# Paired experts: the small expert's up copy and the gated values go ahead of the second up rounding on ScalarE

## The chip, the cores and the metric

The kernel runs on one core of one Trainium2 chip. The metric is the device time of one execution in microseconds; the time before is the median of three runs. Five engines work side by side, each through its own queue in order, and wait for each other by semaphores: TensorE (PE in the profile, PEld for its weight loads), VectorE (DVE), ScalarE (ACT), GpSimd (POOL) and SyncE (SP), which here issues the transfers of the weights.

## The reference

Four layers on 256 tokens of width 1024, in two blocks. The stage that matters here is the mixture of experts in the second layer:

```
def swiglu(x, w1, w3, w2):
    return (jax.nn.silu(x @ w1) * (x @ w3)) @ w2

def moe_swiglu(x, w_router, w1, w3, w2):
    ...
    logits = (t @ w_router).astype(jnp.float32)
    top_val, top_idx = lax.top_k(logits, TOP_K)
    top_w = jax.nn.softmax(top_val, axis=-1)
    combine = jnp.sum(jax.nn.one_hot(top_idx, N_EXPERTS, dtype=jnp.float32) * top_w[..., None], axis=1)
    out = jnp.zeros_like(t)
    for e in range(N_EXPERTS):
        out = out + combine[:, e:e + 1].astype(t.dtype) * swiglu(t, w1[e], w3[e], w2[e])
    return out.reshape(bn, s, d)
```

There are 8 experts with two chosen for each token, and a hidden width of 3584. Every number is float32, so all of an expert's weights come from memory once, whoever uses them: 42 slots of 1 MB for each expert, 336 in all.

## The kernel before

**Pairs and steps.** The experts are handled in four pairs: of each pair one expert has many tokens (up to 128) and one has few (up to 64). The hidden width is cut into 14 chunks of 256 columns, so there are 4 x 14 = 56 steps (`PAIR_STEPS`). In a step s the core needs six slots of weights, 128 x 2048 numbers each: two up slots and one down slot of the "many" expert, and the same of the "few" expert.

**Two ways to multiply.** The few expert's products run in plain float32 on the slots as they lie in the ring. The many expert's run as three products of rounded numbers each: every weight w is split in a high part (w rounded, made by ScalarE into a buffer that the profile calls `work_rounded`) and a low part (w minus the high part, made by VectorE in place in the ring, `ring_rounded`). The same is done with the gated values (`ff_hid_rounded`, high and low part).

**The ring.** SP issues one transfer for each slot into a ring of six (`ring`, L732, `expert_slot`). Before the issue of slot n it waits until TensorE has used slot n - 6, in the order of use; `weights_used` counts the slots that TensorE is done with. The slots of a step stand in the order many up (two halves), few down of the step before, few up (two halves), many down of the step before. The two halves of many up for step s + 1 are the last two of the six that are wanted while step s is under way.

**TensorE**, for a step s, runs in this order (L1896 on, all recorded by helper line L1392, the turn at L1936):

```
                for s in range(1, PAIR_STEPS):
                    many_up(s)
                    few_down(s - 1)
                    few_up_products(s)
                    many_turn(s)
                    many_down(s - 1)
                    few_turn(s)
                    side(s)
```

`many_up` (24 matmuls, two halves of 12; each half needs the low part of its slot, and its end releases the slot), `few_down` and `few_up_products` (`ring` as an operand), `many_turn` (a transpose of the gated values of 128 tokens), `many_down` (12 matmuls with `ff_hid_rounded`), `few_turn` (eight 64-column products of `h_heads,hT`; it waits for the few expert's up copy, `few_up_here`, and for the low part of the gated values, `many_hid_low`), and `side`, which in up to eight of the 14 steps of a pair gathers tokens, turns, or scatters results.

**ScalarE** (`paired_experts`, L1022 on), in the profile's lines: L1052 silu of the few expert (`h_heads`), L1045 high part of the many down slot, L1058 silu of the many expert (`ff_silu`; it waits for the end of `many_up(s)`), L1038 high part of an up slot of step s + 1 (`up_high_of`, once for each half, each waiting for its landing), L1064 the few expert's up products copied out of PSUM (`few_up_of`, tile `hT`; it waits for the end of `few_up_products(s)` and for the few turn of the step before), L1070 high part of the gated values (`hid_high_of`; it waits for `many_turn(s)`).

**VectorE** (`paired_experts`, L2679 on, recorded by helper line L2262) makes the low parts in an order of its own: gated values of the many expert (`ff_mid`), low part of the first up slot of step s + 1 (`ring_rounded`), low part of the gated values (`ff_hid_rounded`), low part of the second up slot, later the few expert's gated values (`h_heads`) and the low part of the many down slot.

The orders are written out by hand, one after the other; no scheduler moves anything. In the printed code `up_high[s % 2][half]`, `down_high`, `few_up`, `ff_hid_r` and `ring_r` are the buffers `work_rounded`, `work_rounded`, `hT`, `ff_hid_rounded` and `ring_rounded` of the profile.

Of the kernel before, what the change touches and what calls it, by code (L numbers as in the profile page):

```python
# [34 lines left out]
PAIR_STEPS = PAIRS * EXPERT_CHUNKS  # L35
# [149 lines left out]
def build_program(nc, x_in, cond_in, params_in, consts_in, stream_in, out, plan=PLAN):  # L185
# [6 lines left out]
    with ExitStack() as ctx:  # L192
# [48 lines left out]
        def bank(i, a=0, b=512):  # L241
            if i in banks:
                return banks[i][:, a:b]
            two, half = (mid, i - 2) if i < 4 else (pair, i - 6)
            return two[:, 512 * half + a:512 * half + b]
# [399 lines left out]
        def pair_used(s, what, half=0):  # L645

            return weights_used, moe_first + pair_slot(s, what) + half + 1

        def pair_here(s, what, half=0):

            at = moe_first + pair_slot(s, what) + half
            return weights_here[at % RING], 16 * (at // RING + 1)

        def pair_ring(s, what, half=0):

            return (moe_first + pair_slot(s, what) + half) % RING
# [214 lines left out]
        def _(act):  # L871
# [150 lines left out]
            def paired_experts():  # L1022
# [11 lines left out]
                def up_high_of(s, half):  # L1034
                    act.wait_ge(*pair_here(s, "many", half))
                    if s >= 2:
                        act.wait_ge(*pair_used(s - 2, "many", half))
                    act.activation(up_high[s % 2][half], ring[:, pair_ring(s, "many", half), :], ACT.Copy)\  # L1038
                       .then_inc(many_up_high, 1)

                def down_high_of(s):
                    act.wait_ge(*pair_here(s, "many_down"))
                    if s >= 2:
                        act.wait_ge(*pair_used(s - 2, "many_down"))
                    act.activation(down_high[s % 2], ring[:, pair_ring(s, "many_down"), :], ACT.Copy)\  # L1045
                       .then_inc(many_down_high, 1)

                def silu_of_few(s):
                    act.wait_ge(few_turned, s + 1)
                    if s >= 2:  # L1050
                        act.wait_ge(few_hid_here, s - 1)
                    act.activation(few_silu[s % 2], bank(6, T, T + P), ACT.Silu).then_inc(few_silu_here, 1)  # L1052

                def silu_of_many(s):
                    act.wait_ge(*pair_used(s, "many", 1))
                    if s >= 2:
                        act.wait_ge(many_hid, s - 1)
                    act.activation(ff_silu[:, s % 2, :], bank(4, 0, T), ACT.Silu).then_inc(many_silu, 1)  # L1058

                def few_up_of(s):  # L1060
                    act.wait_ge(*pair_used(s, "few", 1))
                    if s:
                        act.wait_ge(few_turned, s)
                    act.activation(few_up, bank(5), ACT.Copy).then_inc(few_up_here, 1)  # L1064

                def hid_high_of(s):
                    act.wait_ge(many_turned, s + 1)
                    if s >= 2:
                        act.wait_ge(*pair_used(s - 2, "many_down"))
                    act.activation(ff_hid_r[:, s % 2, :], bank(6, 0, T), ACT.Copy).then_inc(many_hid_high, 1)  # L1070
# [14 lines left out]
                def evacuate_side(s):  # L1085
                    p, c = divmod(s, EXPERT_CHUNKS)
                    if c == 0 and p:
                        outs(p - 1)
                    if c == 7:
                        act.wait_ge(pair_turned, p + 1)  # L1090
                        if p:
                            act.wait_ge(pair_scattered, 4 * p)
                        act.activation(pair_back, bank(7), ACT.Copy).then_inc(pair_backs, 1)
                    if p + 1 < PAIRS and c in (8, 9):
                        many_tokens_of(p + 1, c - 8, 7)
                    if p + 1 < PAIRS and c == 10:
                        few_tokens_of(p + 1, 7)
# [6 lines left out]
                for s in range(PAIR_STEPS):  # L1104
                    if s:
                        silu_of_few(s - 1)
                        evacuate_side(s - 1)
                        down_high_of(s - 1)
                    silu_of_many(s)
                    if s + 1 < PAIR_STEPS:  # L1110
                        for half in range(2):
                            up_high_of(s + 1, half)
                    few_up_of(s)
                    hid_high_of(s)
                silu_of_few(PAIR_STEPS - 1)
                down_high_of(PAIR_STEPS - 1)
                outs(PAIRS - 1)
# [253 lines left out]
            for n, kind in enumerate(plan):  # L1371
                norm(n, 0)
                if kind.startswith("first"):
                    first_mixers(firsts.index(n))
                elif kind == "even":
                    even_mixers(n)
                else:
                    odd_mixers(n)
                norm(n, 1)
                if kind == "first1":  # L1380
                    router(n)
                    paired_experts()
                    with act.If(more_tokens(act)):
                        experts_again()
                    norm(n, 2)
                else:
                    feed_forward(n, kind)
# [1934 lines left out]
```

## Time and profile before

| | us |
|---|---|
| median of 3 runs | 2489.4 (2487.48 to 2495.14) |
| profiled execution, its own time | 2496.13 |
| its span | 2494.3 |
| TensorE busy | 2365.2 (95%) |
| VectorE busy | 1477.3 (59%) |
| ScalarE busy | 970.3 (39%) |
| read from memory | 653.76 MB, mean 263 GB/s over the span |

The busy shares are means over the whole span. Matmuls overlap, so a busy TensorE isn't TensorE at its peak. The stage of the paired experts fills the time from about 600 to 1530 us after the start; in it a row of the timeline gives the start of an instruction, how long it took, its line and tiles, and in brackets how long its engine had been idle and what ended that. A chain of waits is followed back from the last instruction to what released it, step by step.

### The profile page before, as it was taken

How to read it: one execution, taken by the hardware profiler on the slowest of the kernel's cores; microseconds unless marked ns; L12 is line 12 of the kernel's file. 1: busy time of each engine (PE TensorE's matmuls, PEld its weight loads, DVE VectorE, ACT ScalarE, POOL GpSimd, SP SyncE). 2: the span in 40 equal slices, each digit the busy share in tenths (PEclk: the TensorE clock that was granted, in tenths of full speed). 3: DMA queues.
4: the chain of work that ended last, by engine and by line, in shares of the span. 5: the costliest groups of instructions: out<-in, count | busy, mean ns of one | idle time of the engine just before them, and what ended most of it. 6: DMA issues, size and time to landing. Idle time of an engine off the chain costs nothing.

```text
span 2494.3 us, 36105 instructions
## 1 busy us (share of the span) xinstructions
PE 2365.2 (95%) x14484; PEld 1922.5 (77%) x14484; DVE 1477.3 (59%) x1843; ACT 970.3 (39%) x1149; POOL 44.8 (2%) x37
## 2 busy tenths in 40 slices
PE   5999999998999999989999998999999999999999
PEld 4889998876566565656665665779899999997998
DVE  5835885764444454444544444375489887873665
ACT  3214434113434444343434434222434456653332
POOL 0100001000000000000000000010000000000000
PEclk9989999999999999999999999999999999999999
DMA  9845894746989999989989999230488543432452
GB/s 369 330 152 203 358 364 179 304 152 262 366 349 366 368 364 359 364 348 369 363 338 382 362 374 371 107 118 1 154 330 360 210 169 136 149 139 101 155 184 100
DMA packets 90428, 656.78 MB, mean 263 GB/s; under 512 B 10033, under 2 KB 10289, under 8 KB 10801
## 3 DMA queue, kind: packets, MB, share of 16 engines
q1 hardware_dynamic: 80928, 589.34, 61.2%
q10 hardware_dynamic: 9360, 65.52, 6.4%
q8 instruction: 97, 1.59, 0.2%
q14 instruction: 43, 0.34, 0.0%
HBM read 653.76 MB, written 1.05 MB: 263 GB/s over the span
## 4 chain that ended last, share of the span: by engine, by line
PE 78%; DMA 9%; DVE 6%; issue 3%; ACT 3%; ACTq 0%; SPq 0%; DVEq 0%
PE bank L1392 77%; DMA ring<-stream_dram 9%; DVE work L2274 1%; DVE ring_rounded L2262 1%; ACT hT L1064 1%; DVE ff_hid_rounded L2262 1%; DVE rstd L2322 0%; PE bank L1936 0%; DVE xT L2268 0%; ACT ff_hid_rounded L1070 0%; DVE ring L2274 0%; PE bank L1772 0%; DVE ff_mid L2268 0%; ACT work_rounded L1038 0%; DVE yT L2268 0%
## 5 line engine op out<-in xcount | busy, mean ns | idle before, releaser
L2262 DVE TENSOR_TENSOR ring_rounded<-ring,work_rounded 128x2048 fp32r<-128x2048 f32 x264 | 606.4, 2298 | 461.6 <-ACT work_rounded L1045 347.7
L1392 PE MATMUL bank<-work_rounded,proj_rounded 128*128 128x512 f32 x896 | 310.2, 418 | 1.5 <-DVE ring_rounded L2262 1.5
L1392 PE MATMUL bank<-h_heads_rounded,work_rounded 128*128 128x256 f32 x1344 | 278.9, 280 | 0.0
L1392 PE MATMUL bank<-yT_rounded,ring_rounded 128*128 128x256 f32 x960 | 273.6, 285 | 0.0
L1038 ACT ACTIVATE work_rounded<-ring 128x2048 fp32r<-128x2048 f32 x112 | 214.7, 1918 | 131.5 <-DMA ring<-stream_dram 131.0
L1392 PE MATMUL bank<-hT,ring 128*128 128x256 f32 x1088 | 242.9, 383 | 2.0 <-ACT hT L926 2.0
L1392 PEld LDWEIGHTS bank<-hT,ring 128*128 128x128 f32 x1088 | 207.5, 192 | 37.7 <-issue 9.9
L1392 PEld LDWEIGHTS bank<-h_heads_rounded,work_rounded 128*128 128x128 f32 x1344 | 220.6, 189 | 3.0 <-issue 2.9
L1045 ACT ACTIVATE work_rounded<-ring 128x2048 fp32r<-128x2048 f32 x56 | 107.2, 1914 | 286.9 <-DMA ring<-stream_dram 281.5
L1392 PEld LDWEIGHTS bank<-work_rounded,proj_rounded 128*128 128x128 f32 x896 | 177.1, 198 | 42.4 <-issue 2.8
L1392 PE MATMUL bank<-ring,proj 128*64 128x512 f32 x896 | 201.8, 592 | 0.0
L1392 PEld LDWEIGHTS bank<-yT_rounded,ring_rounded 128*128 128x128 f32 x960 | 186.3, 194 | 0.0
L1392 PE MATMUL bank<-ring_rounded,proj_rounded 128*128 128x512 f32 x448 | 182.5, 407 | 0.0
L1392 PEld LDWEIGHTS bank<-ring,proj 128*64 128x64 f32 x896 | 64.2, 137 | 127.5 <-issue 127.4
L1392 PE MATMUL bank<-work_rounded,ff_hid_rounded 128*128 128x512 f32 x448 | 155.6, 408 | 1.9 <-DVE ring_rounded L2262 1.9
L1392 PE MATMUL bank<-yT_rounded,work_rounded 128*128 128x256 f32 x480 | 138.8, 289 | 10.3 <-DVE ring_rounded L2262 10.3
L1392 PE MATMUL bank<-proj_rounded,work_rounded 128*128 128x256 f32 x480 | 138.0, 287 | 0.0
L1392 PE MATMUL bank<-yT_rounded,proj_rounded 128*128 128x256 f32 x480 | 136.1, 284 | 1.5 <-DVE ring_rounded L2262 1.5
L1392 PE MATMUL bank<-proj_rounded 128*128 128x256 f32 x480 | 135.7, 283 | 0.0
L1392 PE MATMUL bank<-h_heads_rounded,ring_rounded 128*128 128x256 f32 x480 | 135.5, 282 | 0.0
L1392 PE MATMUL bank<-yT,ring 128*128 128x256 f32 x512 | 114.1, 380 | 6.6 <-DMA ring<-stream_dram 3.7
L1392 PE MATMUL bank<-hT_rounded,work_rounded 128*128 128x256 f32 x384 | 115.7, 301 | 1.5 <-DVE h_heads_rounded L2268 1.4
(329 smaller groups left out, 4161.7 us busy)
## 6 DMA issues: line engine op xcount, KB each, us to landing
ring<-stream_dram SPq DMA_DIRECT2D x561, 1024.0 KB, 6.9
work<-stream_dram ACTq DMA_DIRECT2D x56, 1024.0 KB, 9.1
params<-params_dram ACTq DMA_DIRECT2D x1, 1728.5 KB, 28.9
consts<-consts_dram ACTq DMA_DIRECT2D x1, 1568.0 KB, 37.7
cond<-cond_dram ACTq DMA_DIRECT2D x2, 512.0 KB, 3.7
xT<-x_dram ACTq DMA_DIRECT2D x1, 1024.0 KB, 10.1
out_dram<-xT SPq DMA_DIRECT2D x1, 1024.0 KB, 3.9
consts<-consts_dram ACTq DMA_DIRECT2D x1, 577.0 KB, 32.2
```

The costliest lines, as they stand in the source:

```text
L1038: act.activation(up_high[s % 2][half], ring[:, pair_ring(s, "many", half), :], ACT.Copy)\
L1045: act.activation(down_high[s % 2], ring[:, pair_ring(s, "many_down"), :], ACT.Copy)\
L1064: act.activation(few_up, bank(5), ACT.Copy).then_inc(few_up_here, 1)
L1392: return pe.matmul(o, lhsT=a, rhs=b, start=start, stop=stop, skip_group_check=True)
L2262: return dve.tensor_tensor(o, a, b, op)
L2274: last = dve.scalar_tensor_tensor(half, half, 1.0, row, ALU.mult, ALU.mult, accum_out=column(h))
```

## The change

In `paired_experts` on ScalarE the rounding of the second up slot of the next step (`up_high_of(s + 1, 1)`) is called after `few_up_of(s)` and `hid_high_of(s)` instead of ahead of them. The first one stays where it was. No other function and no other engine's code is touched.

```
                     if s + 1 < PAIR_STEPS:
-                        for half in range(2):
-                            up_high_of(s + 1, half)
+                        up_high_of(s + 1, 0)
                     few_up_of(s)
                     hid_high_of(s)
+                    if s + 1 < PAIR_STEPS:
+                        up_high_of(s + 1, 1)
                 silu_of_few(PAIR_STEPS - 1)
```

ScalarE in the paired experts, two steps running; a row is one or more instructions of a line, `work_rounded<-ring` at L1038 is the rounding of an up slot, `hT<-bank` the few expert's up copy, `ff_hid_rounded<-bank` the high part of the gated values. Before:

```order
L1058 ACTIVATE ff_silu<-bank 128x256
L1038 ACTIVATE work_rounded<-ring 128x2048 x2
L1064 ACTIVATE hT<-bank 128x512
L1070 ACTIVATE ff_hid_rounded<-bank 128x256
L1052 ACTIVATE h_heads<-bank 128x128
L1045 ACTIVATE work_rounded<-ring 128x2048
```

With the change:

```order
L1058 ACTIVATE ff_silu<-bank 128x256
L1038 ACTIVATE work_rounded<-ring 128x2048
L1064 ACTIVATE hT<-bank 128x512
L1070 ACTIVATE ff_hid_rounded<-bank 128x256
L1038 ACTIVATE work_rounded<-ring 128x2048
L1052 ACTIVATE h_heads<-bank 128x128
L1045 ACTIVATE work_rounded<-ring 128x2048
```

The second of the two roundings moved behind the two reads of PSUM; this repeats in 55 steps.

VectorE at the same place, of the changed kernel (the helper's line is one further down than before, 2263 for 2262): the product `ff_mid`, the low part of the first up slot, the low part of the gated values, the low part of the second up slot.

```order
L2263 TENSOR_TENSOR ff_mid<-bank4,ff_silu 128x256
L2263 TENSOR_TENSOR ring_rounded<-ring,work_rounded 128x2048
L2263 TENSOR_TENSOR ff_hid_rounded<-bank67,ff_hid_rounded 128x256
L2263 TENSOR_TENSOR ring_rounded<-ring,work_rounded 128x2048
L2263 TENSOR_TENSOR h_heads<-bank67,h_heads 128x128
```

Nothing moved here: the order is that of before.

## Rows read from the trace of the kernel before

**Rows 1.** The page: engines' busy time (share of span), and the chain by engine
```profile
PE 2365.2 (95%) x14484; PEld 1922.5 (77%) x14484; DVE 1477.3 (59%) x1843; ACT 970.3 (39%) x1149; POOL 44.8 (2%) x37
...
PE 78%; DMA 9%; DVE 6%; issue 3%; ACT 3%; ACTq 0%; SPq 0%; DVEq 0%
```

**Rows 2.** Windows: the stage, eight full us, a slow clock, an empty queue
```profile
core 0: us, PE busy (x) PEld busy (x) DVE busy (x) ACT busy (x) POOL busy (x), PEclk, DMA share, GB/s
600.00:1530.00 930.00, 880.39 (x4056) 562.29 (x4058) 434.29 (x380) 390.04 (x400) 0.00 (x0) 0.97 0.92 361
1067.00:1075.00 8.00, 5.86 (x30) 4.62 (x29) 5.12 (x4) 3.59 (x5) 0.00 (x0) 1.00 1.01 423
...
1108.00:1112.00 4.00, 4.00 (x16) 3.39 (x15) 1.98 (x2) 0.28 (x1) 0.00 (x0) 0.57 0.74 309
1113.00:1117.00 4.00, 4.00 (x19) 2.56 (x20) 0.71 (x1) 2.18 (x2) 0.00 (x0) 1.00 0.56 215
```

**Rows 3.** Waits from 600 to 1530 us: total us, times, longest
```profile
ACT work_rounded L1038 <- DMA ring<-stream_dram: 124.4, 105, 4.3
...
DVE ff_hid_rounded L2262 <- ACT ff_hid_rounded L1070: 64.3, 54, 2.4
PEld bank L1392 <- ACT hT L1064: 56.9, 28, 4.2
PE bank L1392 <- DVE ff_hid_rounded L2262: 46.5, 30, 4.0
PEld bank L1936 <- DVE ff_mid L2262: 25.8, 24, 2.3
```

**Rows 4.** Chain that ended last, in order of time: start, us, what
```profile
1060.99 7.15 DMA ring<-stream_dram
...
1069.98 0.58 ACT hT L1064
1070.56 0.28 ACT ff_hid_rounded L1070
1070.84 0.02 issue
1070.87 0.44 DVE ff_hid_rounded L2262
...
1071.44 6.77 PE bank L1392 x32
...
1078.37 7.17 DMA ring<-stream_dram
```

**Rows 5.** Timeline of ScalarE in the same step: start, us, instruction, [idle before]
```profile
1065.72 1.92 ACT L1038 ACTIVATE work_rounded<-ring 128x2048 fp32r<-128x2048 f32 x1 [2.87 <-DMA ring<-stream_dram]
1068.16 1.92 ACT L1038 ACTIVATE work_rounded<-ring 128x2048 fp32r<-128x2048 f32 x1 [0.52 <-DMA ring<-stream_dram]
1069.98 0.58 ACT L1064 ACTIVATE hT<-bank 128x512 f32<-128x512 f32 x1
1070.46 0.38 ACT L1070 ACTIVATE ff_hid_rounded<-bank 128x256 fp32r<-128x256 f32 x1
```

**Rows 6.** Timeline of VectorE in the same step
```profile
1067.67 2.29 DVE L2262 TENSOR_TENSOR ring_rounded<-ring,work_rounded 128x2048 fp32r<-128x2048 f32 x1 [2.42 <-ACT work_rounded L1038]
1070.87 0.42 DVE L2262 TENSOR_TENSOR ff_hid_rounded<-bank,ff_hid_rounded 128x256 fp32r<-128x256 f32 x1 [0.90 <-ACT ff_hid_rounded L1070]
1071.21 2.28 DVE L2262 TENSOR_TENSOR ring_rounded<-ring,work_rounded 128x2048 fp32r<-128x2048 f32 x1
```

**Rows 7.** Timeline of TensorE: end of many down, few turn, first matmul of many up
```profile
1068.91 0.39 PE L1392 MATMUL bank<-work_rounded,ff_hid_rounded 128*128 128x512 f32 x1
1071.44 1.08 PE L1392 MATMUL bank<-h_heads,hT 128*128 128x64 f32 x8 [2.14 <-DVE ff_hid_rounded L2262]
1072.32 0.47 PE L1392 MATMUL bank<-work_rounded,proj_rounded 128*128 128x512 f32 x1
```

**Rows 8.** Timeline of ScalarE in a step whose second up slot lands late
```profile
820.87 1.91 ACT L1038 ACTIVATE work_rounded<-ring 128x2048 fp32r<-128x2048 f32 x1 [0.75 <-DMA ring<-stream_dram]
824.83 1.91 ACT L1038 ACTIVATE work_rounded<-ring 128x2048 fp32r<-128x2048 f32 x1 [2.05 <-DMA ring<-stream_dram]
```

**Rows 9.** Timeline of TensorE in that step
```profile
825.43 0.39 PE L1392 MATMUL bank<-work_rounded,ff_hid_rounded 128*128 128x512 f32 x1
828.10 1.74 PE L1392 MATMUL bank<-h_heads,hT 128*128 128x64 f32 x8 [2.28 <-DVE ff_hid_rounded L2262]
829.60 0.77 PE L1392 MATMUL bank<-work_rounded,proj_rounded 128*128 128x512 f32 x1
```

## The prediction

> **What bounds the kernel now.** The page comes first: TensorE is busy for 95% of the span, and the chain that ended last lies 78% on it and 9% on transfers into the ring [rows 1]. Such shares are means over stages with different limits, so the second view is the table of windows. The diff touches the paired experts alone. Their stage runs from about 600 to 1530 us; TensorE is busy there for 880.39 of 930 us, and the DMA engines show a share of 0.92 at 361 GB/s [rows 2]. Two resources near their limits, tied by a ring of six slots: a slot is refilled only when TensorE has used it, and TensorE works only on what has landed and been rounded.
>
> The third view is the list of waits in that stage. TensorE waits 46.5 us in 30 places for `ff_hid_rounded` from VectorE, and its weight loads wait 56.9 us in 28 places for ScalarE's `hT` [rows 3]; both are the same point, the few turn (eight 64-column products), which needs the small expert's up copy (`hT`) and the low part of the gated values. VectorE in turn waited 64.3 us for the high part from ScalarE, and ScalarE's roundings of up slots waited 124.4 us for landings [rows 3]. So a landing that the few turn has no use for holds it up, through the order on ScalarE.
>
> The fourth view, the chain of one stretch, shows that this is a closed loop [rows 4]: 7.15 us from the issue of a slot to its landing, the rounding (shown as issue, as far as 1069.98), the up copy, the high part, the low part, then 6.77 us of TensorE (few turn and the next many up), whose end releases the slot for the next issue, 7.17 us to land, and so on. From 1060.99 to 1078.37 that is 17.4 us a step. TensorE's own work leaves out its 2.14 us wait [rows 7]; without that the step would be 15.2 us.
>
> **The change part by part.** It removes and adds no instruction; it moves the second up rounding behind the up copy and the high part, in 55 steps. No DMA is issued by ScalarE in this loop, and SP's, VectorE's and TensorE's orders stay.
>
> One step in numbers. Before, the roundings start at 1065.72 and 1068.16, the up copy at 1069.98 and the high part at 1070.46 [rows 5]; the low part starts at 1070.87 [rows 6], the few turn at 1071.44 [rows 7]. Counted from the second rounding's start the few turn is at +3.28 us.
> After, the first rounding ends at 1065.72 + 1.92 = 1067.64. The up copy can follow at about 1067.5 (its products are done, since many down has been running), the high part at 1068.0, ending at 1068.4. Now VectorE is late: in its order the low part of the first up slot, 2.29 us from 1067.67 to 1069.96 [rows 6], stands ahead of the gated values' low part. So that starts at 1069.9, and the few turn, 0.57 us behind it as before, at 1070.47. From the first rounding's start the few turn is at +4.75 us. The step gains 1071.44 - 1070.47 = 0.97 us of its 2.14; in general it gains the distance between the two roundings less 1.47 us, and never more than its wait.
>
> That distance is 2.44 us where two slots land back to back, and more where the second lands late: at 820.87 and 824.83 it is 3.96 us [rows 8]. There the few turn would be ready at 820.87 + 4.75 = 825.62, before many down ends at 825.82, and the wait of 2.28 us goes altogether [rows 9].
>
> Sum over the stage. I went through the steps one by one in the timeline: of the waits that stand in one row as 46.5 us, 30 times [rows 3], 19 are longer than 0.95 us with landings back to back and lose about 0.95 each (18.0); nine or ten are shorter and vanish (about 5); two have a late second landing and lose 2.28 and 1.90 (4.2). Together 27 us. About 19 us stay, bound by VectorE's rounding difference behind the first landing.
>
> What of the 27 us reaches the end? It does where the ring's next issue comes earlier and transfers follow. For: behind a long wait the DMA engines run dry, with a share of 0.56 at 215 GB/s, while they move 423 GB/s when slots are queued [rows 2]; at that rate the stage's 361 GB/s x 930 us would take 794 us, so there is room. Against: where slots are queued, an earlier TensorE only waits longer for the same landing. In my pass over the steps 15 us of the 27 fall directly ahead of a stretch with an empty queue, and 12 where one or two slots were still on their way. I take all of the first and two thirds of the second: 15 + 8 = 23 us.
>
> The clock adds to it. Behind some of the waits the granted clock falls to the lower of its two levels, 1.2 GHz: 0.57 on the mean of 1108 to 1112 [rows 2], and the first many-up matmul takes 0.77 us behind the wait at 828.10 [rows 9], against 0.47 us behind the one at 1071.44, which left the clock alone [rows 7]. The stage's mean of 0.97 [rows 2] is 3% of 930 us, some 28 us of TensorE's work. The drops stand behind waits of this kind, which shrink by a third to a half or go. This is bounded by 0 and 28 us; I take 4, near zero, since a wait of 2.14 us at 1071.44 and one of 2.28 us at 828.10 [rows 7, 9] had opposite outcomes.
> The Trainium skill ("TensorE: Matmul & The Clock Gate", HAM oscillation) says that waits for data between bursts bring the lower clock back each time and that shortening them keeps it away; by that rule this term would be nearer to its upper bound. The trace agrees only in part, since the wait of 2.14 us left the clock as it was.
>
> What the move costs. The second rounding now starts behind the high part: at 1068.40 instead of 1068.16 in this step, 0.24 us later, and it ends at 1070.3. VectorE takes it up at 1070.3 instead of 1071.21 [rows 6], because the gated values' low part stands ahead of it there and is now earlier. So the difference is done 0.9 us sooner than now, and the half of many up that reads it comes only 2.9 us after that product's start (it runs from 1072.32 [rows 7] to 1071.44 + 6.77 = 1078.21 [rows 4], in two equal halves). Cost here 0, covered by VectorE's own queue; what it costs without that cover is the first rival of the other sign. The wait for a landing that up copy and high part lose is taken over by the rounding itself, behind which stand now only the small expert's silu, which waits for the few turn anyway, and the down rounding, whose slot lands later still. ScalarE changes its function as often as before.
>
> Sum: 23 + 4 = 27 us. Against the profiled execution, 2496.13 us (span 2494.3), that gives 2469; it lay 6.7 us above the median of the runs shown, 2489.4, and against that the forecast is 2489.4 - 27 = **2462.4 us**.
>
> **The rivals.**
> (a) The transfers set the pace, and the gain is handed back as longer waits for landings. For it: a DMA share of 0.92 [rows 2], and ScalarE waits for the landing at 105 roundings of up slots [rows 3]. Against it: 423 against 361 GB/s, and the empty stretch [rows 2]. Time: unchanged, 2489 (within 5 us). The Trainium skill ("DMA: Bandwidth & Descriptors", Where 436 GB/s comes from) puts the limit of reads from HBM at about 358 GB/s for a core, by which the stage's 361 is already all there is and this rival is certain; the trace does not agree, as 8 us in a row ran at 423 GB/s. I give it 17%.
> (b) The loop itself gets shorter in each stalled step, so that the landings move too and the remaining 19 us of waits shrink as well, and the clock drops go. Loop through the first slot: 17.4 - 0.97 = 16.4 us. Price: 27 + 5 of the remaining waits + 12 of the clock = 44 us, 2445. The rows of the loop speak for it, the PE side work that several steps carry against it. 12%.
> (c) Slower: the second rounding queues behind the high part, which waits for TensorE's many turn. Where that turn is late, because VectorE's product for it is, the rounding of a slot that has long landed is held, then VectorE's difference, then the second half of the next many up. In the step above the difference is done at 1072.6 and needed at 1071.35 + 2.9 = 1074.25, so it decides from a turn that comes 1.7 us later than here. Where it does in one step of four by 0.7 us, 10 us are lost and little gained: 2499. Against it: the turn's weight loads wait 25.8 us in 24 places, 1.1 us on the mean and 2.3 at the longest [rows 3], mostly inside the slack. 5%.
> (d) The move doesn't take effect, because VectorE's first difference always ends after the second rounding would have. The rows exclude it for steps like these (1069.96 against 1070.84 for the end of the high part); it would give 2489, 2%.
>
> **How the numbers follow.** The forecast of 27 us, give or take 12, has 64%; (a) 17, (b) 12, (c) 5, (d) 2. The range: from (b)'s 2445 to just under the median, 2487, which leaves out most of (a)'s upper half and (c). A measurement of this kernel can tell about 0.3%, 7.5 us, from no change: faster than that is 2481.9 or less, the forecast and (b) with a little of (a), 0.77; the same 0.18; slower 0.05.
>
> **What would show it.** In the profile of the changed kernel, over the same stage: TensorE's wait for `ff_hid_rounded` falls from 46.5 us to 15 to 22, with a longest of under 3; the up copy's start follows the first rounding by about 1.8 us, and the few turn the first rounding's start by 4.75 us wherever it waits; VectorE's idle time before the gated values' low part goes nearly to nothing, since it comes straight from the first difference; GB/s of the stage rises from 361 to about 371; granted clock from 0.97 to 0.98. Wrong at its root: the wait shrinks and the stage is as long as before, with longer waits of ScalarE for landings (a); or a new wait of TensorE for `ring_rounded` inside many up (c).

## The result and the profile after

| | us |
|---|---|
| changed kernel, median of 4 runs | 2453.97 (2447.82 to 2459.84) |
| kernel before, median of the 4 runs beside them | 2488.44 (2482.43 to 2495.14) |
| ratio, changed to before | 0.9861, 95% interval 0.9822 to 0.9899 |
| profiled execution of the changed kernel, its span | 2450.09, 2448.3 |

The change takes 34.5 us off, 1.4% (interval 1.0 to 1.8%); 27 were forecast against 2489.4, and the median lies in the range. The two profiled executions differ by more, 2496.13 - 2450.09 = 46 us, since the one of before lay above its median and this one below. A second profile of the same changed kernel is at 2462.11 us (the run `e0_changed_again`, below), 34 us under before's; it is the highest of that run's six times, whose median is 2457.10. Where an amount matters both are given.

First the page of the changed kernel, engines' busy times and the chain by engine, which answer to [rows 1]. (The file is one line longer, so that TensorE's helper line is L1393, the turn L1937 and VectorE's helper L2263.)

```profile
PE 2341.7 (96%) x14484; PEld 1907.9 (78%) x14484; DVE 1475.2 (60%) x1843; ACT 967.9 (40%) x1149; POOL 44.7 (2%) x37
...
PE 72%; DMA 12%; DVE 7%; issue 4%; ACT 4%; ACTq 0%; SPq 0%; DVEq 0%
```

With the same instructions TensorE is busy for 23.5 us less, which shorter waits alone don't explain. Second, windows over the whole stage, from the first many up to the last many down: before, changed, changed again. The columns are those of [rows 2].

```profile
589.00:1562.00 973.00, 914.66 (x4212) 583.66 (x4213) 452.28 (x393) 409.59 (x420) 0.00 (x0) 0.97 0.92 362
```

```profile
587.00:1517.00 930.00, 892.07 (x4208) 570.46 (x4209) 450.57 (x394) 407.30 (x419) 0.00 (x0) 0.99 0.95 378
```

```profile
589.00:1529.00 940.00, 896.78 (x4208) 570.88 (x4208) 450.71 (x393) 406.02 (x419) 0.00 (x0) 0.99 0.95 374
```

The stage went from 973 us to 930 (940 in the second profile). That is 43 of the 46 us between the profiled executions (33 of the 34), so nearly all of the gain is in it. It splits in two: TensorE busy 914.66 to 892.07, 22.6 us less (17.9 in the second), and TensorE idle, length less busy, 58.3 to 37.9, 20.4 us less (15.1 in the second). The granted clock went from 0.97 to 0.99, the transfers from 362 to 378 GB/s (374).

Third, the waits in the changed kernel's stage that answer to [rows 3].

```profile
PEld bank L1937 <- DVE ff_mid L2263: 56.8, 40, 2.7
PE bank L1937 <- DVE ff_mid L2263: 22.7, 27, 1.8
PE bank L1393 <- DVE ff_hid_rounded L2263: 11.3, 13, 3.7
PE bank L1393 <- DVE ring_rounded L2263: 3.3, 3, 1.9
```

Two of the second profile:

```profile
PE bank L1393 <- DVE ff_hid_rounded L2263: 21.7, 23, 3.7
PE bank L1937 <- DVE ff_mid L2263: 18.1, 26, 2.6
```

And three of the kernel before, over the whole stage:

```profile
PE bank L1392 <- DVE ff_hid_rounded L2262: 47.4, 31, 4.0
PE bank L1936 <- DVE ff_mid L2262: 7.4, 11, 1.4
PE bank L1392 <- DVE ring_rounded L2262: 3.4, 3, 1.9
```

The few turn's wait is down from 47.4 us, 31 times, to 11.3 us, 13 times (21.7 us, 23 times, in the second profile), and no weight load waits for `hT` any more (56.9 us in [rows 3]). What grew is the many turn's wait for `ff_mid`: 22.7 us (18.1) in place of 7.4. The chain shows what it hangs on (start, us, what):

```profile
1051.48 8.39 DMA ring<-stream_dram
...
1059.89 1.92 ACT work_rounded L1045
...
1064.04 0.43 DVE ff_mid L2263
...
1064.52 0.44 PE bank L1937 x2
```

A transfer of 8.39 us, the high part of the down slot (L1045), its low part on VectorE (shown as issue), and only behind this, by VectorE's order, the gated values `ff_mid` that the many turn waits for. It is the same pattern one place further on: a landing for which the waiting product has no use, shown here in one step.

One step in the timeline, to set beside [rows 5 to 7]. ScalarE, VectorE, TensorE of the changed kernel:

```profile
1078.83 1.92 ACT L1038 ACTIVATE work_rounded<-ring 128x2048 fp32r<-128x2048 f32 x1 [1.83 <-DMA ring<-stream_dram]
1080.65 0.58 ACT L1064 ACTIVATE hT<-bank 128x512 f32<-128x512 f32 x1
1081.12 0.38 ACT L1070 ACTIVATE ff_hid_rounded<-bank 128x256 fp32r<-128x256 f32 x1
1081.39 1.92 ACT L1038 ACTIVATE work_rounded<-ring 128x2048 fp32r<-128x2048 f32 x1
```

```profile
1080.78 2.29 DVE L2263 TENSOR_TENSOR ring_rounded<-ring,work_rounded 128x2048 fp32r<-128x2048 f32 x1 [1.39 <-ACT work_rounded L1038]
1082.99 0.42 DVE L2263 TENSOR_TENSOR ff_hid_rounded<-bank,ff_hid_rounded 128x256 fp32r<-128x256 f32 x1
```

```profile
1083.55 1.08 PE L1393 MATMUL bank<-h_heads,hT 128*128 128x64 f32 x8 [0.75 <-DVE ff_hid_rounded L2263]
```

The few turn starts 1083.55 - 1078.83 = 4.72 us behind the first rounding (4.75 were forecast), and VectorE's difference is what it waits for, as the prediction had it. Every few turn that waits, except the first, lies at 4.72 or 4.73 us in the timeline of either profile of the changed kernel (the first at 4.71).

Last, where the busy time went. One row of the list of groups, the high-part products of many up, before and changed (count, then busy us and mean ns of one):

```profile
L1392 PE MATMUL bank<-work_rounded,proj_rounded 128*128 128x512 f32 x896 | 310.2, 418 | 1.5 <-DVE ring_rounded L2262 1.5
```

```profile
L1393 PE MATMUL bank<-work_rounded,proj_rounded 128*128 128x512 f32 x896 | 300.7, 407 | 1.5 <-DVE ring_rounded L2263 1.5
```

The same 896 matmuls take 9.5 us less. They are the product behind the few turn, where in [rows 9] the clock had fallen; none of them waited itself but for the 1.5 us in the row.

How much of the 22.6 us is the clock? In the stage, the traces' records of the granted clock have the lower level for 51.2 us in the kernel before, for 10.2 us in the changed one and for 13.7 in its second profile. At half the speed, 41 us less of it give back about 20 us (19 in the second profile; both are estimates from these lengths), which accounts for nearly all of the 22.6 us and for the 17.9. Each of the twelve drops of the kernel before begins behind a wait of TensorE of 1.5 to 4.0 us. The other runs agree: the mean granted clock of a whole execution was 0.975 to 0.983 in the 41 runs of the kernel before, with times from 2503.91 down to 2477.54 us, and 0.983 to 0.987 in the ten of the changed one. The means are 0.9797 and 0.9854, which over 2490 us is an estimated 14 us of the 34.5. The kernel before was profiled at 0.978, below its mean, so the profiles show the clock's part somewhat larger than the medians do.

Busy time isn't the clock alone: the few turn reads 1.08 us behind a wait [rows 7] and 1.00 without one, as in this row of the changed kernel's timeline. For 30 waits that is an estimated 2 us.

```profile
1051.14 1.00 PE L1393 MATMUL bank<-h_heads,hT 128*128 128x64 f32 x8
```

### The profile page after: what moved, and what is told of

It is laid out like the page before. It is cut to its first block, busy times and chain, and to the rows that moved or that the text cites. A ratio compares the mean times of both kernels' runs of the same rounds, so it can differ in the third digit from the quotient of the medians.

```text
span 2448.3 us, 36105 instructions
## 1 busy us (share of the span) xinstructions
PE 2341.7 (96%) x14484; PEld 1907.9 (78%) x14484; DVE 1475.2 (60%) x1843; ACT 967.9 (40%) x1149; POOL 44.7 (2%) x37
## 4 chain that ended last, share of the span: by engine, by line
PE 72%; DMA 12%; DVE 7%; issue 4%; ACT 4%; ACTq 0%; SPq 0%; DVEq 0%
PE bank L1393 71%; DMA ring<-stream_dram 11%; ACT work_rounded L1045 2%; DVE ring_rounded L2263 2%; DVE work L2275 1%; PE bank L1937 1%; ACT work_rounded L1038 1%; DMA work<-stream_dram 1%; DVE rstd L2323 1%; DVE ff_mid L2263 0%; DVE ff_mid L2269 0%; DVE xT L2269 0%; DVE ring L2275 0%; PE bank L1773 0%; DVE yT L2269 0%
## 5 line engine op out<-in xcount | busy, mean ns | idle before, releaser
L2263 DVE TENSOR_TENSOR ring_rounded<-ring,work_rounded 128x2048 fp32r<-128x2048 f32 x264 | 607.1, 2301 | 490.2 <-ACT work_rounded L1045 386.0
L1393 PE MATMUL bank<-work_rounded,proj_rounded 128*128 128x512 f32 x896 | 300.7, 407 | 1.5 <-DVE ring_rounded L2263 1.5
L1393 PE MATMUL bank<-h_heads_rounded,work_rounded 128*128 128x256 f32 x1344 | 279.0, 280 | 0.0
L1393 PE MATMUL bank<-yT_rounded,ring_rounded 128*128 128x256 f32 x960 | 273.7, 285 | 0.0
L1393 PE MATMUL bank<-hT,ring 128*128 128x256 f32 x1088 | 243.3, 384 | 2.0 <-ACT hT L926 2.0
L1038 ACT ACTIVATE work_rounded<-ring 128x2048 fp32r<-128x2048 f32 x112 | 214.7, 1917 | 61.8 <-DMA ring<-stream_dram 61.5
L1045 ACT ACTIVATE work_rounded<-ring 128x2048 fp32r<-128x2048 f32 x56 | 107.1, 1913 | 329.1 <-DMA ring<-stream_dram 329.0
L1393 PEld LDWEIGHTS bank<-hT,ring 128*128 128x128 f32 x1088 | 207.8, 192 | 37.8 <-issue 9.8
L1393 PEld LDWEIGHTS bank<-h_heads_rounded,work_rounded 128*128 128x128 f32 x1344 | 220.4, 189 | 3.0 <-issue 2.9
L1393 PE MATMUL bank<-ring,proj 128*64 128x512 f32 x896 | 201.8, 592 | 0.0
L1393 PEld LDWEIGHTS bank<-work_rounded,proj_rounded 128*128 128x128 f32 x896 | 170.2, 190 | 40.1 <-issue 2.7
L1393 PEld LDWEIGHTS bank<-yT_rounded,ring_rounded 128*128 128x128 f32 x960 | 186.3, 194 | 0.0
L1393 PE MATMUL bank<-ring_rounded,proj_rounded 128*128 128x512 f32 x448 | 177.6, 396 | 0.0
L1393 PEld LDWEIGHTS bank<-ring,proj 128*64 128x64 f32 x896 | 64.2, 137 | 127.5 <-issue 127.4
L1393 PE MATMUL bank<-work_rounded,ff_hid_rounded 128*128 128x512 f32 x448 | 156.6, 411 | 1.9 <-DVE ring_rounded L2263 1.9
L1393 PE MATMUL bank<-yT_rounded,work_rounded 128*128 128x256 f32 x480 | 138.8, 289 | 10.8 <-DVE ring_rounded L2263 10.8
L1393 PE MATMUL bank<-proj_rounded,work_rounded 128*128 128x256 f32 x480 | 138.0, 287 | 0.0
L1393 PE MATMUL bank<-yT_rounded,proj_rounded 128*128 128x256 f32 x480 | 136.1, 284 | 0.8 <-DVE ring_rounded L2263 0.7
L1393 PE MATMUL bank<-proj_rounded 128*128 128x256 f32 x480 | 135.7, 283 | 0.0
L1393 PE MATMUL bank<-h_heads_rounded,ring_rounded 128*128 128x256 f32 x480 | 135.5, 282 | 0.0
L1393 PE MATMUL bank<-yT,ring 128*128 128x256 f32 x512 | 114.1, 380 | 5.9 <-DMA ring<-stream_dram 3.0
L1393 PE MATMUL bank<-hT_rounded,work_rounded 128*128 128x256 f32 x384 | 115.7, 301 | 1.5 <-DVE h_heads_rounded L2269 1.4
```

The lines of the kernel that those rows point to most:

```text
L1393: return pe.matmul(o, lhsT=a, rhs=b, start=start, stop=stop, skip_group_check=True)
L2263: return dve.tensor_tensor(o, a, b, op)
```

## The experiments

The theory (A): the few turn is held through a closed loop, from the release of the second up slot over its landing and rounding to the few turn and the next many up; the change takes the rounding out of it. Rivals: B, one of the two moved reads alone is the cause; T, the transfers set the pace; and rivals named with the single runs. Ratios are to the kernel before on the same chip, with 95% intervals.

**The changed kernel again.**

> The changed kernel once more, beside the others on the same chip: 2450 to 2460 us, ratio 0.984 to 0.990.

Measured: 2457.10 us, ratio 0.9865 (0.9835 to 0.9894). As expected; its profile is the second one above.

**Each half of the change alone.** First only the up copy:

```
                         up_high_of(s + 1, 0)
                     few_up_of(s)
-                    hid_high_of(s)
                     if s + 1 < PAIR_STEPS:
                         up_high_of(s + 1, 1)
+                    hid_high_of(s)
```

> Of the change only the few expert's up copy goes ahead of the second up rounding; the high part of the gated values stays behind it. The few turn needs both. Theory A (the few turn is held by whichever of the two comes last, so a landing stays in its way): the high part now starts 1.9 us after the second rounding's start, the low part 0.4 later, the few turn at about +2.8 us instead of +3.28, so 0.5 us saved in each of 30 waits at the most: 2475 to 2487 us. Rival B (it is the up copy's wait of 56.9 us for weight loads that mattered): nearly all of the gain, 2455 us.

Measured: 2471.32 us, ratio 0.9921 (0.9892 to 0.9951). Then only the high part:

```
                         up_high_of(s + 1, 0)
-                    few_up_of(s)
                     hid_high_of(s)
                     if s + 1 < PAIR_STEPS:
                         up_high_of(s + 1, 1)
+                    few_up_of(s)
```

> Of the change only the high part of the gated values goes ahead of the second up rounding; the few expert's up copy stays behind it. Theory A: the low part is ready early, but the up copy still starts 1.82 us after the second rounding, takes 0.58, and the few turn follows 0.15 to 0.2 later, at +2.6 instead of +3.28: 0.7 us saved in each of 30 waits at the most, 2467 to 2483 us. VectorE isn't held before its second difference, as in the whole change. Rival B (it is VectorE's order, freed by the early high part, that mattered, not the few turn's wait): nearly all of the gain, 2455 us.

Measured: 2460.65 us, ratio 0.9885 (0.9855 to 0.9914). Both ranges of theory A were missed on the fast side. The kernel before took 2492.97 us beside these, so the up copy alone brings 21.7 us, the high part alone 32.3 and the two together 35.9. For the up copy alone rival B falls. For the high part alone its time does not fall: 2460.65 us (runs from 2456.65 to 2463.12) can't be told from the whole change's 2457.10 (2453.03 to 2462.11), and "nearly all of the gain" is what was measured. The waits have to decide between A and B there. The stage's window and TensorE's waits of each, first the up copy alone, then the high part alone:

```profile
588.00:1543.00 955.00, 904.86 (x4210) 572.26 (x4211) 452.00 (x394) 409.40 (x419) 0.00 (x0) 0.99 0.94 368
```

```profile
PE bank L1393 <- DVE ff_hid_rounded L2263: 36.1, 29, 4.0
```

```profile
588.00:1527.00 939.00, 901.48 (x4208) 567.76 (x4209) 450.22 (x394) 409.94 (x419) 0.00 (x0) 0.99 0.95 374
```

```profile
PE bank L1393 <- ACT hT L1064: 22.8, 28, 1.6
PE bank L1393 <- DVE ff_hid_rounded L2263: 3.7, 1, 3.7
```

With the up copy alone the stage is 18 us shorter, of which TensorE's idle time (955 - 904.86 = 50.1) gives 8 us and its busy time (914.66 - 904.86) 10. With the high part alone it is 34 us shorter, 21 from idle and 13 from busy. The few turn's waits there went from 47.4 to 22.8 + 3.7 = 26.5 us, 21 less, which is A's 0.7 us for each of 30 waits. The wait inside many up that an earlier second difference on VectorE, B's cause, could shorten was only 3.4 us before and is 3.3 us here. So A's mechanism holds and B's doesn't, and what made A's ranges too slow is the busy time. The lower clock stands for 20.5 and 10.2 us of these two stages, against 51.2 before. That would give back 15 and 20 us (estimates as above), 5 to 7 us more than the busy time fell by; what took that difference isn't settled.

**The change in half of the steps.**

```
                     if s + 1 < PAIR_STEPS:
                         up_high_of(s + 1, 0)
+                        if s >= PAIR_STEPS // 2:
+                            up_high_of(s + 1, 1)
                     few_up_of(s)
                     hid_high_of(s)
-                    if s + 1 < PAIR_STEPS:
+                    if s + 1 < PAIR_STEPS and s < PAIR_STEPS // 2:
                         up_high_of(s + 1, 1)
```

> The change in the first 28 of the 56 steps alone. Theory A: gain in proportion, half of 33 us, 2472 to 2480; in the trace the few turn's waits of the first half are as in the changed kernel and those of the second half as before. Rival S (the start of the stage, where the pipeline gets its lead, is what matters): nearly all of the gain from the first half, under 2465.

Measured: 2471.19 us, ratio 0.9938 (0.9908 to 0.9969), about half of the whole gain and 0.8 us below A's range. The few turn's wait in the first and in the second half of the stage (up to 1060 us and from there):

```profile
PE bank L1395 <- DVE ff_hid_rounded L2265: 7.4, 8, 3.7
```

```profile
PE bank L1395 <- DVE ff_hid_rounded L2265: 18.2, 17, 2.1
```

In the changed kernel the halves have 9.0 and 2.3 us, in the kernel before 25.6 and 21.7. So the first half waits as in the changed kernel and the second nearly as before, as A has it. Rival S falls; the effect adds up step by step and isn't a lead won once.

**A quarter of the bytes taken away**, from the kernel before and from the changed one. The few expert's slots arrive by half, so these two kernels leave out part of that expert's weights and serve for the time alone:

```
+                    few_rows = SLOT // 2 if what.startswith("few") and 2 <= s < PAIR_STEPS - 1 else SLOT
-                    sp.dma_start(ring[:, (moe_first + n) % RING, :],
-                                 stream_in[bass.ds(first_of[e] + part, 1)].rearrange("a p n -> p (a n)"))\
+                    sp.dma_start(ring[:, (moe_first + n) % RING, 0:few_rows],
+                                 stream_in[bass.ds(first_of[e] + part, 1)].rearrange("a p n -> p (a n)")[:, 0:few_rows])\
```

> The kernel before, with the second half of each of the few expert's slots not transferred (steps 2 to 54): 128 x 1024 numbers instead of 128 x 2048, so that the few expert's products use stale weights. A quarter of the stage's bytes is gone, everything else stands. Theory A (a closed loop of latencies: release of the second up slot by TensorE, transfer, rounding, up copy, high part, low part, few turn, many up): the loop does not go away with the bytes. The second up slot lands no sooner than 4.7 us after its issue, the few turn comes 3.28 us after that, so TensorE still waits about 0.9 us in nearly every step without side work: 15 to 35 us of waits left for the few turn, stage about 925 to 945 us. Rival T (the waits before are bandwidth): the few turn's waits go nearly to nothing, stage under 915 us.

Measured: 2436.52 us, ratio 0.9791 (0.9758 to 0.9824).

> The changed kernel with the same transfers left out (second half of each of the few expert's slots, steps 2 to 54; stale weights in its products). Theory A: with the loop through the second up slot cut and bytes to spare, the few turn's wait is nearly gone (the first up slot lands at about 2.0 us behind many up's end, and 2.0 + 4.75 = 6.8 is ahead of many down's end at 7.2), and the many turn's wait too: faster than the light kernel before by 20 to 40 us. Rival T: the same time as the light kernel before within 5 us, since nothing is left that the order on ScalarE could hold.

Measured: 2421.44 us, ratio 0.9729 (0.9697 to 0.9761). Stage and TensorE's wait, light before, then light changed:

```profile
589.00:1512.00 923.00, 896.29 (x4211) 571.31 (x4212) 452.87 (x394) 411.04 (x420) 0.00 (x0) 0.99 0.81 291
```

```profile
PE bank L1393 <- DVE ff_hid_rounded L2263: 20.0, 16, 4.0
```

```profile
587.00:1490.00 903.00, 887.64 (x4208) 570.50 (x4209) 452.28 (x394) 410.92 (x419) 0.00 (x0) 1.00 0.82 297
```

```profile
PE bank L1394 <- DVE ff_hid_rounded L2264: 7.9, 7, 3.7
```

With bytes to spare (291 GB/s where 423 were seen [rows 2]) the few turn still waits 20.0 us, inside A's 15 to 35, and the change is still worth 2436.5 - 2421.4 = 15 us. So the wait doesn't need crowded transfers alone, against T. But T has a share: of the 47.4 us, 27.4 went with the bytes, the 16 waits left are far from A's "nearly every step", and the stage of 923 us lies between A's 925 and T's 915. The difference was to be 20 to 40 us by A and under 5 by T, and lies between as well: less than half of the change's gain (34.5) is left when the transfers are light. That the rest exists only where a ring near its rate meets a TensorE that issues late is my reading; no run separates the two.

**How far the rounding can go back.** The changed kernel with the second rounding one place later still, behind the small expert's silu:

```
                         silu_of_few(s - 1)
+                        up_high_of(s, 1)
                         evacuate_side(s - 1)
...
                     hid_high_of(s)
-                    if s + 1 < PAIR_STEPS:
-                        up_high_of(s + 1, 1)
```

> The changed kernel with the second up rounding moved on by one more place, behind the small expert's silu, which waits for the few turn. It measures the slack that the prediction's slower case rests on. The rounding then starts at about 9.2 us behind many up's end and ends at 11.1, VectorE's difference at 13.4; TensorE wants it at 11.1 in a step without side work. Theory A: TensorE waits about 2 us for the second half in some 35 steps without much side work: 50 to 90 us slower than the changed kernel, 2505 to 2545 us, with a new wait for ring_rounded inside many up. Rival T (transfers set the pace): under 2480.

Measured: 2488.84 us, ratio 1.0012 (0.9990 to 1.0034). All of the gain is gone. TensorE's waits in the stage (total, times, longest):

```profile
PE bank L1392 <- DVE ring_rounded L2262: 55.4, 35, 1.9
...
PE bank L1392 <- DVE ff_hid_rounded L2262: 7.3, 6, 3.7
```

Its stage, in the windows:

```profile
590.00:1554.00 964.00, 898.35 (x4209) 565.92 (x4208) 449.84 (x393) 405.99 (x419) 0.00 (x0) 1.00 0.94 365
```

The new wait is the one that A named, inside many up, in 35 places of about 1.6 us each, while the few turn hardly waits. A's price of 50 to 90 us was too high: it is 35 us, 2488.8 - 2454.0. The wait itself, 55.4 us, is in that range, but other waits are shorter than in the changed kernel (the few turn's 7.3 us against 11.3, the many turn's 2.0 against 22.7). T, under 2480 us, falls too. In the changed kernel itself this wait is 3.3 us in 3 places, as before: the slack of the prediction's rival (c) is real and the change stays inside it, but it is only one place wide. The window tells something more: TensorE is idle for 65.7 us here, more than in the kernel before, and yet the granted clock is 1.00. Most of these are waits of at most 1.9 us (55.4 us in 35 places); before, the few turn's 46.5 us went up to 4.0 us each [rows 3]. That points to the long waits, not to their sum, as what brings the clock down. Length alone doesn't decide it either, as two waits of TensorE show, of the kernel before and of this one:

```profile
878.86 1.33 PE L1392 MATMUL bank<-h_heads,hT 128*128 128x64 f32 x8 [1.54 <-DVE ff_hid_rounded L2262]
```

```profile
624.83 0.51 PE L1392 MATMUL bank<-work_rounded,proj_rounded 128*128 128x512 f32 x1 [1.64 <-DVE ring_rounded L2262]
```

The clock fell behind the first (granted 0.50 at 880 to 882 us) and not behind the second, and here not behind any wait of that length; the one drop of this stage stands behind the wait of 3.7 us near its start. In the kernel before it fell behind seven of TensorE's nine idle stretches above 2 us, and behind five of 1.5 to 1.9 us. What sets these apart stays open.

**Both roundings behind the reads**, with the low part of the gated values first on VectorE (that edit is the second of the two moves on VectorE below; here is the one on ScalarE):

```
+                    few_up_of(s)
+                    hid_high_of(s)
                     if s + 1 < PAIR_STEPS:
-                        up_high_of(s + 1, 0)
-                    few_up_of(s)
-                    hid_high_of(s)
-                    if s + 1 < PAIR_STEPS:
-                        up_high_of(s + 1, 1)
+                        for half in range(2):
+                            up_high_of(s + 1, half)
```

> The kernel with the low part of the gated values first on VectorE, and on ScalarE both up roundings behind the up copy and the high part, so that no landing of an up slot stands ahead of the few turn. Theory A: the few turn never waits, but the first rounding now starts at 5.0 us behind many up's end instead of about 2, its difference ends at 9.2, and TensorE wants it at 8.1: about 1 us of wait at the start of many up in the steps without side work, 15 to 45 us slower than with the first rounding ahead, 2460 to 2490 us. Rival U (the fewer landings ahead of the few turn, the better): 2445 us or less.

Measured: 2463.05 us, ratio 0.9913 (0.9879 to 0.9948), in A's range; rival U falls.

```profile
PE bank L1392 <- DVE ring_rounded L2262: 40.7, 37, 1.9
...
PE bank L1392 <- DVE ff_hid_rounded L2262: 1.0, 1, 1.0
```

The few turn never waits but once, and many up waits 40.7 us for its low parts instead. The kernel with the same order on VectorE and the first rounding ahead took 2446.07 us beside it (`e11_low_first_again`, below), so the first rounding's move costs 17 us. Taking every landing out of the few turn's way isn't better than taking out the one that isn't needed yet.

**What is late next: two moves on VectorE.** First the gated values ahead of the down slot's low part, which is what the chain above asks for:

```
                         side(s - 1)
-                        down_low_of(s - 1)
                     hidden_of_many(s)
+                    if s:
+                        down_low_of(s - 1)
```

> The changed kernel, and on VectorE the many expert's gated values (ff_mid) ahead of the low part of the down slot of the step before. In the changed kernel's trace the many turn waits for ff_mid: weight loads 55.4 us in 39 places, transposes 21.8 us in 26, and ff_mid stands behind a difference of 2.29 us that stands behind a landing. Theory A: with TensorE's waits set by such orders, the turn's 21.8 us go but for 3 or so; many down needs the low part 0.7 us later than the turn needs ff_mid, so part of the wait moves there: 8 to 15 us faster than the changed kernel, 2439 to 2446. Rival T (the stage is now bound by the transfers, 0.95 of the DMA engines' time): within 4 us of the changed kernel, the wait reappears at many down or at the few turn.

Measured: 2453.06 us, ratio 0.9857 (0.9825 to 0.9888), beside 2457.10 us of the changed kernel on the same chip: no difference that can be told. TensorE's waits:

```profile
PE bank L1393 <- DVE ring_rounded L2263: 17.8, 26, 1.9
...
PE bank L1937 <- DVE ff_mid L2263: 0.9, 1, 0.9
```

The turn's wait is gone and has come back as 17.8 us in 26 places, 16.2 us of them ahead of many down, which needs the same late landing. T holds for this wait, and A, which forecast 8 to 15 us, does not. Second, the gated values' low part ahead of the first up slot's low part:

```
                     hidden_of_many(s)
+                    hidden_low(s)
                     if s + 1 < PAIR_STEPS:
                         up_low_of(s + 1, 0)
-                    hidden_low(s)
```

> The changed kernel, and on VectorE the low part of the gated values ahead of the low part of the first up slot, which is what bound the few turn by my sum. Theory A: the few turn's wait goes, but the first up slot's low part is now ready at 8.2 us behind many up's end or later where TensorE wants it at 8.1, so the wait moves into the start of the next many up: no gain, 0 to 15 us slower than the changed kernel, 2457 to 2475. Rival V (VectorE's order is the next limit and can be lifted): 5 to 10 us faster than the changed kernel, under 2452.

Measured: 2445.89 us, ratio 0.9828 (0.9790 to 0.9866).

> Once more the changed kernel with the low part of the gated values ahead of the low part of the first up slot on VectorE, beside the others on one chip: 2443 to 2449 us, 8 to 12 us under the changed kernel.

Measured: 2446.07 us, ratio 0.9842 (0.9813 to 0.9871), in the range. Stage and waits of the first of the two runs, `e6_low_first`:

```profile
588.00:1511.00 923.00, 890.39 (x4207) 571.36 (x4208) 446.77 (x394) 406.38 (x419) 0.00 (x0) 1.00 0.97 381
```

```profile
PE bank L1937 <- DVE ff_mid L2263: 20.3, 30, 1.5
...
PE bank L1393 <- DVE ring_rounded L2263: 9.6, 14, 1.9
...
PE bank L1393 <- DVE ff_hid_rounded L2263: 2.2, 1, 2.2
```

For `e6_low_first` I had expected the wait to move into many up and cost up to 15 us. It moved there by 6 us only (9.6 against 3.3) while the few turn gave back 9 to 19 (11.3 or 21.7 to 2.2), so V's side was right. Its nine runs lie between 2443.57 and 2449.82 us, the ten of the changed kernel between 2447.82 and 2462.11. By the ratios (0.9828 and 0.9842 against 0.9861 and 0.9865) that would be 5 to 9 us beyond the change, but their intervals overlap and the two were not timed side by side, so a second gain is likely and not settled. Both moves together:

> The changed kernel with both moves on VectorE: the gated values (ff_mid) ahead of the low part of the down slot, and the low part of the gated values ahead of the low part of the first up slot. Theory A: the many turn's 20 us of waits of the second alone move to many down for the most part, as they did in the first alone: 0 to 6 us faster than the second alone, 2440 to 2446. Rival T: the same time as the second alone.

Measured: 2449.63 us, ratio 0.9861 (0.9833 to 0.9889), no better than the second alone (2446.07 beside it) and above A's 2440 to 2446; rival T's equal time fits, within the spread of the runs (2444.10 to 2456.84). The many turn's wait went to many down here too, which waits 15.9 us for its low parts.

## Why the prediction was right, and where its sizes were off

*What bounds the kernel.* Right. The few turn's wait was the one to take away: the halves of the change and the change in half of the steps move the time with it.

*The step's sum.* Right to 0.03 us: +4.72 us behind the first rounding, VectorE's difference as the next bound. VectorE's wait for the high part went from 64.3 us [rows 3] to 1.2 over the same window, as forecast. The sum over the stage, 27 us off and about 19 left, gave 11.3 us left in one profile and 21.7 in the other. The longest was to be under 3 us and is 3.7, in the stage's first few turn.

*What reaches the end, 23 us of waits.* Too high, by 3 us in one profile and 8 in the other. TensorE's idle time fell by 20.4 us (15.1 in the second). The split of the 27 us by empty and filled queues, 15 and two thirds of 12, was tested by no run. What was handed back has a name that the prediction didn't give: the many turn behind VectorE's low part of the down slot, up 15.3 us (10.7). The prediction asked only what the few turn waits for next, and not who else waits for a landing once TensorE is early.

*The clock, 4 us.* The mis-sized term. Busy time fell by 22.6 us (17.9) for the same instructions, nearly all of it by the clock. The bound of 28 us was right, the choice near zero was not: I took it from one pair of waits of like length with opposite outcomes. The halves show that a saving of 8 us of idle time already came with 10 us of busy time. Here the Trainium skill ("TensorE: Matmul & The Clock Gate", HAM oscillation) was the better guide: it says that waits for data between bursts bring the lower clock back. The trace agrees, with 0.97 before and 0.99 after, but not for every wait: 35 waits of about 1.6 us went with 1.00.

*The total.* 27 us were forecast, 34.5 measured. By the profiles the two terms miss in opposite directions, the waits 3 to 8 us too high and the clock 14 to 19 us too low, and partly cancel. That the total is so much closer than its clock term is luck: with 18 to 23 us there the same sum would have given 41 to 46 us, more than the 34.5 of the medians.

*The costs of the move, 0.* Right: the wait for `ring_rounded` is 3.3 us, against 3.4 before. Rival (c) is measured by the rounding moved once more, which costs 35 us.

*The rivals.* The result lies between the forecast (27) and rival (b) (44), whose mechanism, landings that move along and a clock that stays up, is what happened in part: the stage's rate rose to 374 to 378 GB/s where 371 was expected. Rival (a) does not hold for the change, since the rate rose and the light kernels still differ, though by less than half of its gain, so the transfers have a part in it; it does hold for the next wait in line, as the gated values moved first show.

## What to carry to other kernels

On an engine that works in order, a wait for a transfer holds everything behind it, so put what another engine is waiting for ahead of what only prepares the next step, and stop at the place where that preparation becomes the late one: putting the two reads ahead of the rounding was worth 34 us here, nearly all of it by the high part's move alone, and putting the next instruction ahead of it too cost it all. Price a wait of TensorE at more than its length when the granted clock beside it has fallen, and look for who else waits for the same landing, since the gain from the next reordering may only change the name of the waiting product.

## What the runs showed that I had not expected

- TensorE's own work got shorter by 18 to 23 us in the stage without a change to any of its instructions, about as much as its waits did.
- Of two reads that both had to come earlier, one alone (the high part) brought 32.3 of 35.9 us and the other alone 21.7: the parts of such a change don't add up.
- With a quarter of the bytes gone the kernel before is 51 us faster and the changed one 33 us faster than with all of them (2454.0 to 2421.4), so neither is free of the transfers.
- Taking away the many turn's wait (22.7 and 18.1 us in the two profiles) brought nothing that can be told, since it came back at many down, while taking away the few turn's (11.3 and 21.7) may have brought 5 to 9 us: what a wait is worth isn't read from its length.
